# Moving the slots of the adaLN modulation tasks, and summing layer 0's first modulation on TensorE in 32-column strips

## The reference, cut to what matters

```
for i in range(DEPTH):
    mod = silu(c) @ ada_w[i] + ada_b[i]                 # (1024) @ (1024, 6144)
    sh1, sc1, g1, sh2, sc2, g2 = jnp.split(mod, 6)
    h = rms_norm(x, norm_mix[i]) * (1.0 + sc1) + sh1
    y = dilated_attention(h, ...) if i % 2 == 0 else hgrn2_mixer(h, ...)
    x = x + g1 * y
    h = rms_norm(x, norm_ffn[i]) * (1.0 + sc2) + sh2
    x = x + g2 * ((silu(h @ w1) * (h @ w3)) @ w2)
```

## Time and profile before

| | us |
|---|---|
| median of 3 runs (lowest, highest) | 852.24 (850.59, 853.17) |
| the profiled execution's own time | 851.94 |
| its span | 850.1 |
| TensorE busy | 820.1 (96%) |
| VectorE busy | 603.7 (71%) |
| ScalarE busy | 435.8 (51%) |
| GpSimd busy | 121.3 (14%) |

### The profile page before, as it was taken

How to read it: one execution, slowest core, us unless ns; L and a number is a source line. 1 busy time by engine, 2 the same in 40 slices (tenths; PEclk the granted TensorE clock), 3 DMA queues, 4 the chain that set the end, 5 groups by cost and what they waited for, 6 DMA issues and landing times.

```text
span 850.1 us, 12071 instructions
## 1 busy us (share of the span) xinstructions
PE 820.1 (96%) x4800; PEld 676.4 (80%) x4800; DVE 603.7 (71%) x745; ACT 435.8 (51%) x558; POOL 121.3 (14%) x154
## 2 busy tenths in 40 slices
PE   4999999989999999999999999999999999999998
PEld 2778888877878887888887887888788888887886
DVE  4897898768789777567666776778688756644544
ACT  5265454444545467344334456786686644334431
POOL 3000111111111100001010000376730000000000
PEclk9899999999999999999999999999999999999999
DMA  9997888877988734788888745444345567765531
GB/s 323 366 357 261 293 260 276 292 224 223 277 266 268 251 122 168 226 265 271 277 279 259 263 156 191 150 150 149 122 155 168 192 198 235 252 215 166 181 99 50
DMA packets 122107, 189.05 MB, mean 222 GB/s; under 512 B 5683, under 2 KB 91048, under 8 KB 122052
## 3 DMA queue, kind: packets, MB, share of 16 engines
q1 hardware_dynamic: 109796, 146.10, 52.9%
q0 software_dynamic: 12256, 42.18, 15.0%
HBM read 187.18 MB, written 1.09 MB: 221 GB/s over the span
## 4 chain that ended last, share of the span: by engine, by line
PE 72%; DVE 9%; DMA 5%; POOL 4%; issue 4%; ACT 3%; SPq 2%; DVEq 0%; POOLq 0%; ACTq 0%
PE bank L516 64%; POOL arena L410 3%; DMA ada_w<-in_ada_w_dram 3%; PE bank L756 2%; POOL arena L409 2%; SPq L309 1%; PE bank L730 1%; DVE acc L1436 1%; DVE wlo L1415 1%; DMA raw<-in_attn_w_qkv_dram 1%; PE bank L873 1%; DMA x<-in_x_dram 1%; PE bank L711 1%; PE bank L594 1%; SPq L300 1%
## 5 line engine op out<-in xcount | busy, mean ns | idle before, releaser
L1415 DVE TENSOR_TENSOR wlo<-raw,whi 128x2048 fp32r<-128x2048 f32 x120 | 275.3, 2298 | 44.4 <-ACT whi L1010 44.3
L1010 ACT ACTIVATE whi<-raw 128x2048 fp32r<-128x2048 f32 (+1 forms) x124 | 235.6, 1902 | 24.2 <-DMA raw<-in_attn_w_qkv_dram 15.3
L516 PE MATMUL bank<-whi,hT_hi 128*128 128x512 f32 (+1 forms) x728 | 196.4, 394 | 2.0 <-DVE arena L1666 1.2
L516 PE MATMUL bank<-wlo,hT_hi 128*128 128x512 f32 (+1 forms) x752 | 195.0, 383 | 0.0
L516 PE MATMUL bank<-whi,hT_lo 128*128 128x512 f32 (+1 forms) x728 | 187.1, 381 | 0.0
L516 PEld LDWEIGHTS bank<-wlo,hT_hi 128*128 128x128 f32 x752 | 138.5, 190 | 28.1
L516 PEld LDWEIGHTS bank<-whi,hT_hi 128*128 128x128 f32 x728 | 130.3, 189 | 31.8 <-issue 7.3
L516 PEld LDWEIGHTS bank<-whi,hT_lo 128*128 128x128 f32 x728 | 133.0, 189 | 26.3
L1436 DVE SCALAR_TENSOR_TENSOR acc<-ada_w,cact,acc 128x1024 f32<-128x1024 f32 x80 | 102.3, 1279 | 16.7 <-DMA ada_w<-in_ada_w_dram 14.8
L393 POOL DMA_DIRECT2D ada_w<-in_ada_w_dram x80 | 42.6, 532 | 496.8 <-DVE acc L1436 479.6
L1255 ACT ACTIVATE arena<-bank 128x256 f32<-128x256 f32 x44 | 14.5, 381 | 165.4 <-PE bank L516 165.4
(11 more groups left out here) (187 smaller groups left out, 797.7 us busy)
## 6 DMA issues: line engine op xcount, KB each, us to landing
raw<-in_ffn_w_dram SPq DMA_DIRECT2D x88, 512.0 KB, 4.9
ada_w<-in_ada_w_dram POOLq DMA_DIRECT2D x80, 512.0 KB, 5.0
raw<-in_attn_w_qkv_dram SPq DMA_DIRECT2D x62, 512.0 KB, 6.5
raw<-in_ffn_w_dram SPq DMA_DIRECT2D x22, 1024.0 KB, 5.0
raw<-in_hgrn_w_in_dram SPq DMA_DIRECT2D x16, 1024.0 KB, 5.4
arena<-in_ada_w_dram SPq DMA_DIRECT2D x16, 512.0 KB, 9.9
raw<-in_attn_w_qkv_dram SPq DMA_DIRECT2D x4, 1024.0 KB, 7.5
raw<-in_attn_w_out_dram SPq DMA_DIRECT2D x4, 1024.0 KB, 6.6
```

What stands on the lines that cost most here:

```text
L516: mm = nc.tensor.matmul(dst[t][c][:, 0:n], lhs[:, k0 + k, t * P:(t + 1) * P], w[:, k, c * 512:c * 512 + n], start=start and k == 0, stop=s ...
L1010: return nc.scalar.activation(dst, src, ACT.Copy)
L1415: nc.vector.tensor_tensor(wlo[:, m % RAW, :], raw[:, m % RAW, :], fp(hi_of(m)), ALU.subtract).then_inc(s["split"], 1)
```

## The change

Five parts; the core of the diff stands below.

1. Layer 0's first modulation is summed by TensorE: for each of eight chunks of the first half and four of the second, four strips of 32 columns by 256 accumulate in PSUM. Four chunks of the second half (`SUMMED = 4`) stay on VectorE. The result is copied and turned by two transposes.
2. The opening's order: the second and third unit's loads lie elsewhere among the chunks, unit 3 is loaded, rounded and split in parts, the second half of the input is scaled partly on ScalarE, and the products of unit 3 are reordered.
3. For units 3 to 8, `qk_rsqrt` and `qk_normalise` of the step before now come ahead of `round_unit` and `split_unit` of the step.
4. In the attention, of two `ada_op`s of a step only the first stays ahead of `att_normalise`; the others follow `qk_normalise`.
5. Fewer `ada_op`s in the attention (40 in place of 48; 32 in place of 24 in the FFN), and other steps for the tasks; turns are always two steps after the sum.

```
-ADA_FFN0 = 8 * KC
+ADA_FFN0 = 7 * KC
+        cact32 = acc[:, 0, 256:512].rearrange("p (k o) -> p k o", o=32)
...
             first_load(KC)
             load_unit(1)
-            for n in range(KC + 1, KC + 5):
+            first_load(KC + 1)
+            first_load(KC + 2)
+            load_unit(2)
+            for n in range(KC + 3, 2 * KC):
                 first_load(n)
-            load_unit(2)
-            for n in range(KC + 5, 2 * KC):
-                first_load(n)
-            for m in range(3, UNITS):
+            load_by_halves(3)
+            for m in range(4, UNITS):
...
                     if blk < 4:
-                        pool.wait_ge(s["mod_red"], blk - 1)
+                        pool.wait_ge(s["mod_red"], 2)
...
             def turn_task(r):
                 pe.wait_ge(s["ada_copy"], QUARTERED.index(r) + 1)
+                if pv[0]:
+                    pe.wait_ge(s["ot_ev"], pv[0])
+                pv[1] = r + 1
...
+            def quarters(dst, left, right, start, stop):
+                for r in range(4):
+                    mm = nc.tensor.matmul(dst[32 * r:32 * r + 32, 0:256], left, right[:, r * 256:(r + 1) * 256],
+                                          start=start, stop=stop)
+                return mm
+
+            def first_chunk(n, start=False, stop=False):
+                half, k = divmod(n, KC)
+                pe.wait_ge(first_in[n], 16)
+                mm = quarters(bank[7 if half else 3], cact32[:, k, :], first_w[k], start, stop)
+                mm.then_inc(s["first_mm"], 1)
...
+                if m == 2:
+                    first_chunk(2 * KC - 2)
+                    pe.wait_ge(s["first_sum"], SUMMED)
+                    quarters(bank[7], ones[:, 0:32], acc[:, 1], False, False)
+                    first_chunk(2 * KC - 1, stop=True)
                 pe.wait_ge(s["xn_lo"], 2 * half + 2)
                 product(hT_lo, w[0], 1, False, False)
                 if m == 2:
-                    first_reduce(1, bank[7])
+                    first_columns(1, bank[7])
...
             pe.wait_ge(s["h0_raw"], 4)
+            for k in range(SUMMED, KC - 2):
+                first_chunk(KC + k, start=k == SUMMED)
             half_unit(2)
...
             for m in range(2, PURE):
+                if m < QU and qk_last(m - 1) is not None:
+                    qk_normalise(qk_last(m - 1))
                 split_unit(m + AHEAD)
...
-                for n in range(ada_done(m - 1), ada_done(m)):
+                sums = range(ada_done(m - 1), ada_done(m))
+                for n in sums[:1]:
                     ada_op(n)
                 if pr >= 1 and j % 2 == 0 and j < 8:
                     att_normalise(J)
-                if qk_last(m - 1) is not None:
+                if pr and qk_last(m - 1) is not None:
                     qk_normalise(qk_last(m - 1))
+                for n in sums[1:]:
+                    ada_op(n)
...
 def tasks_at(m):
-    late = {3: [7], 14: [8], 15: [9], 23: [10]}
-    return {12: [0], 14: [1], 20: [2], 24: [3], 27: [4], 28: [5], 33: [6]}.get(m, []) + late.get(m - M_FFN0, [])
+    late = {3: [6], 12: [7], 17: [8], 18: [9], 25: [10]}
+    return {12: [0], 14: [1], 19: [2], 25: [3], 30: [4], 32: [5]}.get(m, []) + late.get(m - M_FFN0, [])
 
 def turns_at(m):
-    after = 1 if m < M_FFN0 else 2
-    return [r for r in tasks_at(m - after) if r in QUARTERED]
+    return [r for r in tasks_at(m - 2) if r in QUARTERED]
...
 def ada_done(m):
-    return 2 * KC + max(0, m - 5) * 8 // 5
+    return 2 * KC + max(0, m - 5) * 4 // 3
```

More of the change, by code:

```diff
@@ L309, in load_unit, with load_by_halves @@
                     sp.dma_start(slot[:, :, c0:c0 + n], src).then_inc(raw_in[m % RAW], 16)
+            def load_by_halves(m):
+                for k in range(0, 4, 2):
+                    for src, nk, c0, n in pieces(m):
+                        slot = raw[:, m, :].rearrange("p (k n) -> p k n", k=nk)
+                        sp.dma_start(slot[:, k:k + 2, c0:c0 + n], src[:, k:k + 2, :]
+                                     ).then_inc(raw_in[m] if k else s["half3_in" if m else "half_in"], 16)
             sp.dma_start(rows[0:KC, :], a["c"].rearrange("a (k d) -> (a k) d", d=P)).then_inc(s["c_in"], 16)
@@ L1101, in _, with round_halves, second_half_tile, affine @@
                          bank[4 + 2 * t + g][:].rearrange("p (k t) -> p k t", k=4)).then_inc(s["h0_raw"], 1)
[L1102 to L1107, removed]
+            def round_halves(m):
+                act.wait_ge(s["half3_in" if m else "half_in"], 32)
+                copy(whi[:, m, 0:UNIT // 2], raw[:, m, 0:UNIT // 2]).then_inc(s["half_rounded"], 1)
+                if m == 0:
+                    act.wait_ge(s["tab_mm"], 1)
+                    copy(tabT, bank[2][0:GH, 0:TABLE]).then_inc(s["tab_cp"], 1)
+                act.wait_ge(raw_in[m], 32)
+                copy(whi[:, m, UNIT // 2:], raw[:, m, UNIT // 2:]).then_inc(s["rounded"], 1)
+            def second_half_tile():
+                def affine(dst, kc):
+                    return nc.scalar.activation(dst[:, kc, P:2 * P], hT[:, kc, P:2 * P], ACT.Identity,
+                                                bias=first_shift(kc), scale=mod_a[:, 0, 0, kc:kc + 1])
+                act.wait_ge(s["mod_ev"], 2)
+                for kc in range(4, KC):
+                    i = affine(hT_hi, kc)
+                i.then_inc(s["h0_aff_s"], 1)
+                act.wait_ge(s["h0_aff_s"], 1)
+                act.wait_ge(s["xn_hi"], 3)
+                for kc in range(4, KC):
+                    i = affine(hT, kc)
+                i.then_inc(s["xn_hi"], 1)
+            round_halves(0)
             first_round(0, 0)
@@ L1452, in first_modulation @@
             def first_modulation(half):
+                b = bank[7 if half else 3]
+                dve.wait_ge(s["first_mm"], 2 * KC - SUMMED if half else KC)
+                nc.vector.tensor_copy(acc[:, half, 0:256], b[:, 0:256]).then_inc(s["mod_copy"], 1)
                 dve.wait_ge(s["mod_red"], half + 1)
                 at = 48 if half else 56
[L1456 to L1465, removed]
+                bias_cols = cols[:, BIAS0:BIAS0 + 2 * KC].rearrange("p (w h r i) -> p w h r i", w=2, h=2, i=2)[:, :, half]
+                out = small[:, at:at + KC].rearrange("p (w r i) -> p w r i", w=2, i=2)
+                parts = b[:, 256:512].rearrange("p (i w r x) -> p w r i x", i=2, w=2, x=32)[:, :, :, :, 0]
+                nc.vector.tensor_tensor(out, parts, bias_cols, ALU.add).then_inc(s["mod_sum"], 1)
+                dve.wait_ge(s["mod_sum"], half + 1)
                 scale_gain(0, 0, small[:, at + 4:at + 8], 4 * half, 4).then_inc(s["mod_ev"], 1)
```

125 lines of the change are left out of this document (67 added, 58 removed).

## The result

| | before | changed |
|---|---|---|
| time, median of 4 (us) | 852.7 (850.6 to 854.0) | 845.96 (845.66 to 846.37) |
| span of the profiled execution | 850.1 | 843.8 |
| granted clock, mean | .992 | .996 |

The changed kernel is faster by 0.7%: ratio 0.9931, 95% interval 0.9917 to 0.9945. Timed again, it gave 846.34 against 851.48, ratio 0.9932 (0.9920 to 0.9945).

A forecast was written before the change was run, and what follows sets the result against it. TensorE was taken as the bound from 100 to 470 us, DMA at 46.7 to 61. Terms -0.7 - 6.7 - 1.5 + 1.1 + 3.1 + 1.5 = -3.2 us against 851.94 gave 848.7, stated as 848.9; range 843.5 to 852.8.

The forecast's parts named there:

- Opening, -0.7: Parts 1 to 3, up to unit 6: it starts at 65.0 in place of 65.70, 0.7 us won.
- I let unit 5's load land at 51.0 as before: Opening: the same chunks and units still cross full DMA queues, so unit 5's load lands no earlier than 51.0.
- rival (d): Opening: unit 5's load lands earlier than 51.0, up to 2 us more won, 847; chance 0.08.
- The strips: Unit 2 on TensorE: five groups of four strips at 0.9 us each, 2.7 us more after the removed products.
- rival (c): Opening: TensorE drains between strips too, 2.3 us a group, +6.5 us, 855.2; chance 0.07.
- Attention, -6.7: Parts 4 and 5, 100 to 300 us: TensorE's 7.2 us of waits go, except about 0.5 us.
- Rival (b): Attention: the waits come back elsewhere, half the gain (3.4 us) lost, 852.1, no change; chance 0.20.
- The clock in the attention, -1.5: Attention, 188.0 to 191.5 us: the low clock behind the 2.22 us wait goes with it, 1.5 us won.
- Step 17, +1.1: First FFN: TensorE waits 1.1 us ahead of task 8 for the last sum of block 8.
- Step 28, +3.1: First FFN: TensorE's unit 28 waits for VectorE's copy of task 10 and starts 3.1 us late.
- Rival (a): First FFN: the new waits don't come, copy or last sum of block 8 is in time, 843.0; chance 0.20.
- Its clock, +1.5: First FFN, behind the wait of unit 28: the clock falls as after the 2.22 us wait, 1.5 us lost.

The follow-up runs named there:

- experiment 5: The kernel before, with GpSimd's first two modulation chunks held back until unit 5's load has landed: 851.89 us, ratio 1.0002.
- experiment 9: The kernel before with parts 4 and 5 alone, the opening as before: 848.43 us, ratio 0.9966.
- experiment 6: The changed kernel with part 4 undone, both sums of a step ahead of the normalise again: 847.11 us, ratio 0.9947.
- experiment 1: The changed kernel with task 10 summed in FFN step 24 and turned in 26, one step earlier: 841.99 us, ratio 0.9875.
- experiment 2: The changed kernel with three unread products on TensorE ahead of the wait of FFN unit 28: 844.57 us, ratio 0.9900.
- experiment 3: The changed kernel with the FFN's sums spread over steps 3 to 28 in place of 4 to 28: 846.10 us, ratio 0.9915.
- experiment 7: The changed kernel with part 3 undone, rounding and split again ahead of root and normalise for units 3 to 8: 849.34 us, ratio 0.9971.
- experiment 11: The changed kernel timed again, with nothing changed: 846.34 us against 851.48, ratio 0.9932.
- experiment 4: The changed kernel with parts 4 and 5 undone, the opening (parts 1 to 3) kept: 853.38 us, ratio 1.0006.
- experiment 8: The changed kernel with task 10 in FFN steps 24 and 26 and the FFN's sums from step 3 on: 840.85 us, ratio 0.9874.
- experiment 10: Experiment 8 with one unread product behind the one-column products of the recurrence's task 11: 841.75 us, ratio 0.9881.

## Why the prediction came out as it did

- **Opening, -0.7: mis-sized, -2.36 measured.** The step that failed is "I let unit 5's load land at 51.0 as before". It landed before 48.4, since ScalarE's two roundings run from 46.52 to 50.23 without a stop; GpSimd's first two chunks are issued at 44.67. That is rival (d), and experiment 5 shows its mechanism in the kernel before. The second half of the step, "unit 3 starts near 46.7", failed as well: it started at 44.66. The first product came at 23.15 for 25.62, and the clock was up in unit 0, where it had been low before (0.54 in 24 to 31.1 us): no step of mine had that, since my rows start at 46.7. Whether the strips or the changed places of the products for nothing keep it up was not tried. Both halves had to fail for the gain: experiment 5 has the early load alone, and there the end of unit 3 holds the squares. The chain itself is 9.7 us by the trace; by my steps it was 9.8 (55.17 to 65.0). I had sized the chain right and its start wrong; but with its start earlier TensorE's own work ends 0.04 us ahead of it (63.25 and 63.29), so the chain is no longer the only bound.
- **The strips.** I charged 0.9 us a group. Three groups back to back start at 40.00, 40.46 and 40.89, 0.45 us apart, so the idle time on either side comes once for the three; rival (c) with 2.3 a group is refuted. What I had not charged are the two waits for chunks, 1.26 us.
- **Attention, -6.7: close.** The waits are gone as forecast, -7.07 of idle time. The 0.5 us of "such waits remain somewhere" did not come. The clearing did meet a small operation in step 22 (1.20 us for 0.16), but TensorE lost only 0.10 us in that window. The Trainium skill, "SBUF — State Buffer", SBUF: two separate sides, gives the shared ports to whichever of the two starts first, for its whole instruction. In both cases here VectorE's operation ends 0.03 to 0.04 us behind the clearing (1.37 beside 0.97 and 1.20 beside 0.98), which agrees; but by the recorded starts VectorE came first, by 0.36 and 0.19 us, and that the rule does not explain. By the rule alone this cost 1 us; at most 0.10 of it arrives at TensorE. Rival (b) is refuted; experiment 9 puts the gain to parts 4 and 5, and by experiment 6 the order inside a step is 1.4 us of waits in it.
- **The clock in the attention, -1.5: right.** It is 1.00 in 150 to 200 us.
- **Step 17, +1.1: 0.79.** The engine and the line are right.
- **Step 28, +3.1: 2.85.** Experiments 1 and 2 show both cause and cure. Rival (a) is refuted.
- **Its clock, +1.5: right for the profiled execution, not in each.** The wait of 2.85 us is in six traces, with the same products ahead of it; the lower level followed in the changed kernel and in experiments 3 and 7, and not in 6, 9 and 11. The term was a chance, and I had put it in as a certainty.

So the sum was off by 3.1 us in spans (-6.3 for -3.2): the opening by -1.7, the attention by -0.4 (-7.07 for -6.7) and the -0.7 that I can't place there, steps 17 and 28 by -0.3 and -0.25, and +0.2 lost behind them.

One thing no step of mine had: opening and slots are not independent terms. With the old slots the opening's lead is gone by 187 us (experiment 4), where a chunk that TensorE's work hangs on took 3.3 us longer to land; with the new slots it stays. The sum got by with independent terms only because the change makes both.

Two figures of the prediction don't follow from its own terms. Rival (b) says that most of the 7.2 us hang on one late chunk, where the attention's list puts 3.2 us to it. And the 0.03 in the chance for faster has no source, as (b) was to lie wholly above 849.7.

Part of the hit is width and not insight: the measured time is nearer to rival (d) at 847, which had a chance of 0.08, than to the sum, and that rival is what happened to the load.

## What to carry to other kernels

A small copy that another engine waits for belongs in a step where the copying engine is not itself held by the end of the unit ahead; one figure in a table of steps was worth 4.0 us here. A lead won early can be lost at the next place where the work hangs on a load: in experiment 4 the buffer was freed and cleared earlier by the whole lead, and the chunk behind them still landed later than before. So judge an early gain together with the loads that it moves, and give a needed chunk steps of slack, as the new slots do. Before you take away a bound, ask what else ends within a microsecond of it: of two that coincide, removing one gives nothing.

## What was not expected of the hardware

- TensorE's clock after a short pause is not a fixed function of the pause. It fell after waits of 1.95, 2.22 and 5.62 us; after 2.85 us it fell in three traces of six. It also fell behind 1.8 us of one-column products and a wait of 0.35 in the recurrence, in most kernels here, but not in experiments 1 and 2. In the kernel before it also stood at the lower level for most of 24 to 31 us, behind 3.7 us of one-column products, and not in the changed kernel. One fall costs about 1.5 us, but not where VectorE sets the pace right behind it (experiments 1 and 2).
- GpSimd's transfer delays a load on SP's queue while the DMA share is at 1.09: unit 5's load takes 11.3 us beside it and 8.7 without it (experiment 5).
- A modulation chunk takes 5.3 us from issue to landing in one kernel and 8.6 in another that issues it 2.5 us earlier (experiment 4); another one takes 4.2 and 5.3 us in two executions (experiments 8 and 10).
